# The first feed-forward of a two-block kernel: root refinement moved into the long product, left unit's low half ahead of the weight sums, halves of the token sums one chunk later, seven pairs with sums in place of eight

## The reference, cut to what matters

```python
x = x + h                                      # x: (256, 1024)
h = rms_norm(x, norm2_g)                       # row root of mean square, gain norm2_g
x = x + jnp.square(jax.nn.relu(h @ w_ff1)) @ w_ff2      # w_ff1: (1024, 4096), w_ff2: (4096, 1024)
```

## Time and profile before

| | |
|---|---|
| median of three runs | 1223.64 us |
| the profiled execution | 1223.52 us |
| its span | 1221.7 us |
| mean granted clock of TensorE | 0.998 |
| PE busy | 1207.2 us, 99% |
| POOL busy | 862.1 us, 71% |
| ACT busy | 679.6 us, 56% |
| DVE busy | 673.9 us, 55% |
| first product, second product of the first block | 334.8 to 431.1 us, 431.1 to 517.7 us |

### The profile page before, as it was taken

How to read it: one execution, slowest core, us unless ns; L and a number is a source line. 1 busy time by engine, 2 the same in 40 slices (tenths; PEclk the granted TensorE clock), 3 DMA queues, 4 the chain that set the end, 5 groups by cost and what they waited for, 6 DMA issues and landing times.

```text
span 1221.7 us, 18529 instructions
## 1 busy us (share of the span) xinstructions
PE 1207.2 (99%) x7367; PEld 1044.6 (85%) x7367; DVE 673.9 (55%) x1161; ACT 679.6 (56%) x915; POOL 862.1 (71%) x373
## 2 busy tenths in 40 slices
PE   9999999999998999999999999999999999999998
PEld 8987888888887887799999888888879878888877
DVE  6847456341356689756662154536653674544855
ACT  6873757655476566446554464444556666444533
POOL 7977468659876720867579788883776648998194
PEclk9999999999999999999999999999999999999999
DMA  9755355437655655655466776665658435676461
GB/s 304 204 165 171 105 153 170 141 106 223 205 155 147 184 184 195 206 164 159 127 175 214 255 202 184 195 188 160 213 160 283 139 109 170 189 206 189 165 214 69
DMA packets 147773, 218.33 MB, mean 179 GB/s; under 512 B 9392, under 2 KB 79591, under 8 KB 147687
## 3 DMA queue, kind: packets, MB, share of 16 engines
q1 hardware_dynamic: 144295, 209.92, 56.6%
q10 hardware_dynamic: 3392, 7.23, 1.8%
HBM read 216.08 MB, written 1.05 MB: 178 GB/s over the span
## 4 chain that ended last, share of the span: by engine, by line
PE 81%; DVE 10%; POOL 4%; ACT 3%; issue 1%; DMA 0%; SPq 0%; DVEq 0%; ACTq 0%
PE acc L2273 14%; PE acc L2310 8%; PE acc L2312 8%; PE acc L2311 8%; PE acc L2280 7%; PE pm L2326 5%; POOL wlo L640 4%; PE acc L2317 4%; PE acc L2319 4%; PE acc L2320 4%; DVE wlo L1698 2%; PE acc L2239 2%; DVE XT L1726 2%; PE acc L2240 2%; PE acc L2241 2%
## 5 line engine op out<-in xcount | busy, mean ns | idle before, releaser
L640 POOL TENSOR_TENSOR wlo<-raw,whi 128x1024 fp32r<-128x1024 f32 (+4 forms) x366 | 856.8, 2374 | 347.1 <-ACT whi L654 237.2
L654 ACT ACTIVATE whi<-raw 128x1024 fp32r<-128x1024 f32 (+4 forms) x404 | 402.2, 1020 | 211.2 <-PE acc L2280 50.1
L2273 PE MATMUL acc<-XT,whi 128*128 128x512 f32 x960 | 231.7, 393 | 4.5 <-DVE f1r L1741 4.3
L2273 PEld LDWEIGHTS acc<-XT,whi 128*128 128x128 f32 x960 | 177.4, 189 | 40.2 <-DVE f1r L1741 4.7
L2280 PEld LDWEIGHTS acc<-XT,wlo 128*128 128x128 f32 x960 | 123.4, 191 | 4.8
L2280 PE MATMUL acc<-XT,wlo 128*128 128x256 f32 x960 | 124.8, 283 | 0.0
L2310 PE MATMUL acc<-whi,XT 128*128 128x512 f32 (+4 forms) x296 | 112.6, 380 | 0.1
L2317 PE MATMUL acc<-XT,whi 128*128 128x256 f32 x392 | 111.9, 285 | 0.0
L2319 PE MATMUL acc<-XT,whi 128*128 128x256 f32 x392 | 110.9, 283 | 0.0
L2320 PE MATMUL acc<-XT,wlo 128*128 128x256 f32 x392 | 110.9, 283 | 0.0
L2312 PE MATMUL acc<-whi,XT 128*128 128x512 f32 (+4 forms) x296 | 110.0, 372 | 0.0
(11 more groups left out here) (537 smaller groups left out, 2290.8 us busy)
## 6 DMA issues: line engine op xcount, KB each, us to landing
raw<-in_w_in SPq DMA_DIRECT2D x68, 512.0 KB, 4.3
raw<-in_w_ff SPq DMA_DIRECT2D x64, 512.0 KB, 3.8
raw<-in_w_gate SPq DMA_DIRECT2D x44, 512.0 KB, 3.8
raw<-in_w_up SPq DMA_DIRECT2D x44, 512.0 KB, 3.9
raw<-in_w_down SPq DMA_DIRECT2D x44, 512.0 KB, 3.8
raw<-in_w_in_mix SPq DMA_DIRECT2D x36, 512.0 KB, 3.7
raw<-in_w_branch SPq DMA_DIRECT2D x16, 512.0 KB, 4.0
raw<-in_w_out_mix SPq DMA_DIRECT2D x16, 512.0 KB, 3.4
```

Of the source, the lines that this page charges most:

```text
L640: nc.gpsimd.tensor_tensor(piece(wlo, u), piece(raw, u), piece(whi, u).bitcast(F32), ALU.subtract).then_inc(S["w_lo"], 1)
L654: return nc.scalar.activation(out_, in_, func, **k)
L2273: T.matmul(acc[:, n % 2, f, :], piece(whi, u)[:, i, f * P:(f + 1) * P], XT[:, :, k, :], start=k == 0, stop=False)
```

## The change

Four edits, all but one in the first block's feed-forward:

- `SUMS["f2"]` has seven pairs, (2, 4, 5, 7, 9, 10, 12), where it had eight, (2, 3, 5, 6, 8, 9, 11, 12).
- In the loop over the chunks of the first product, `split_sums` of a chunk stands behind the two instructions that read out the next chunk.
- The refinement of the root leaves this loop and stands in the second product, behind the low halves of pair 3.
- In `mixed_lows`, for all three stages, the low half of the left unit is made ahead of the weight sums. Since a left unit's `raw` slot is still read by the sums then, SP waits for one low half more before it reloads such a slot.

```diff
-SUMS = {"f2": (2, 3, 5, 6, 8, 9, 11, 12), "fd0": (2, 3, 5), "fd1": (2, 3, 5)}
+SUMS = {"f2": (2, 4, 5, 7, 9, 10, 12), "fd0": (2, 3, 5), "fd1": (2, 3, 5)}
...
-                    sp_.wait_ge(S["w_lo"], u - RAW + 1)
+                    sp_.wait_ge(S["w_lo"], u - RAW + (2 if u - RAW + 1 in sum_rights else 1))
...
-            def mixed_lows(stage):
+            def mixed_lows(stage, between=None):
...
                     if p not in SUMS[stage]:
                         low_half(left)
                         low_half(right)
+                        if between is not None and p == SUMS[stage][0] + 1:
+                            between()
                         continue
                     g = SUM_FIRST[stage] + SUMS[stage].index(p)
+                    low_half(left)
                     v.wait_ge(S["w_hi"], right + 1)
...
-                    low_half(left)
                     low_half(right, slice(1, UK))
...
+            made = None
             for c in range(DFF // HW):
...
-                if c == 7:
-                    v.wait_ge(S["rstd"], 2)
-                    link(half_variance(0, NT, ss[:, 0:NT], D, 1e-6))
-                    refine_columns(0, NT)
...
                 link(V.tensor_copy(f1r[:], accB(f"f1_{c}", 1)))
                 V.tensor_tensor(f1r[:], accB(f"f1_{c}", 0), f1r[:], ALU.add).then_inc(evac_at(f"f1_{c}")[0], 1)
+                if made:
+                    split_sums(*made)
                 v.wait_ge(S["f1_hi"], c + 1)
                 made = token_sums("f2", c, f1s) if c in SUMS["f2"] else None
                 V.tensor_tensor(FFlo[:, 2 * c:2 * c + 2, :], f1s, FFhi[:, 2 * c:2 * c + 2, :].bitcast(F32),
                                 ALU.subtract).then_inc(S["f1_lo"], 1)
-                if made:
-                    split_sums(*made)
-            mixed_lows("f2")
+            if made:
+                split_sums(*made)
+
+            def squared_roots():
...
+            mixed_lows("f2", squared_roots)
```

More of the change, by code:

```diff
@@ L1733, in _ @@
                     v.wait_ge(S["f1_hi"], c)
-                if c == 7:
-                    v.wait_ge(S["rstd"], 2)
-                    link(half_variance(0, NT, ss[:, 0:NT], D, 1e-6))
-                    refine_columns(0, NT)
-                    link(V.tensor_tensor(rs[:, 8:8 + NT], rs[:, 0:NT], rs[:, 0:NT], ALU.mult))
-                    link(V.tensor_scalar(rs[:, 8 + NT:8 + 2 * NT], rs[:, 8:8 + NT], -1.0, None, ALU.mult))
                 link(V.tensor_copy(f1r[:], accB(f"f1_{c}", 1)))
                 V.tensor_tensor(f1r[:], accB(f"f1_{c}", 0), f1r[:], ALU.add).then_inc(evac_at(f"f1_{c}")[0], 1)
+                if made:
+                    split_sums(*made)
                 v.wait_ge(S["f1_hi"], c + 1)
@@ L1745, in _ @@
                                 ALU.subtract).then_inc(S["f1_lo"], 1)
-                if made:
-                    split_sums(*made)
-            mixed_lows("f2")
+            if made:
+                split_sums(*made)
+            def squared_roots():
+                v.wait_ge(S["rstd"], 2)
+                link(half_variance(0, NT, ss[:, 0:NT], D, 1e-6))
+                refine_columns(0, NT)
+                link(V.tensor_tensor(rs[:, 8:8 + NT], rs[:, 0:NT], rs[:, 0:NT], ALU.mult))
+                link(V.tensor_scalar(rs[:, 8 + NT:8 + 2 * NT], rs[:, 8:8 + NT], -1.0, None, ALU.mult))
+            mixed_lows("f2", squared_roots)
             def folded(t, c, bank):
```

## The result

The changed kernel has a median of 1214.57 us over six runs (1214.50 to 1214.66), the kernel before 1223.68 beside it (1223.36 to 1224.08): 9.1 us less, a ratio of 0.9926, 95% interval 0.9913 to 0.9938. The profiled execution took 1214.64 us with a span of 1212.5.

What follows compares the result with a forecast made beforehand. PE was taken to bound the kernel, busy 99%, losing 10.55 us in two products to waits for late DVE. First product -6.41 and second -3.16 gave -9.6: 1213.9 profiled, 1214.0 median, range 1213.0 to 1216.5.

Steps and rivals of the forecast that it cites:

- two large terms: The first product was to lose 6.41 us and the second 3.16 us, the latter with 0.68 of extra matmuls included.
- The split costs nothing: First product: DVE's split needs 1.3 us and fits in the 1.91 us in which it waits for ACT.
- First product, -6.41: First product: 6.41 us lost to PE's long wait, slow matmuls behind it and a later wait would all go.
- both causes: First product: DVE's 1.5 to 3 us of lag from the sums and the refinement's 3.33 us together broke the allowed lateness.
- The distance of 4.1 us: First product: DVE may be 4.1 us late (5.57 - 1.4) before PE notices.
- Slow clock, 1.71 of it: First product: 16 matmuls behind the long wait took 5.36 us for 3.65, 1.71 lost at granted clock 0.50.
- The refinement costs 1.44 in its new place: Second product: 3.33 us less a 2.04 first instruction read as a wait for POOL, plus 0.15; upper bound 3.33.
- Seven pairs, +0.68, and 66.3 for all thirteen: Second product: 0.68 us more matmuls, thirteen pairs in 66.3 us against 69.42, with 0.3 waited in pair 12.
- Left low half first, and SP's wait: nothing: Pairs with sums: the 1.14 us delay of the sums stays hidden with 0.4 to spare; the later slot costs nothing.
- The rival of the transfers: Second product: second transfers land late, so pairs 10 and 12 wait; 2.4 us more, 1216.4; chance 0.12.
- the slower one: Three stages: the left low half's 1.14 us shows in all 13 sums pairs, 14.8 us, so 1228.8; chance 0.04.
- fd0 and fd1, within 0.3: Stages fd0 and fd1: no waits listed, same count, reordered lows only; change 0, within 0.3 us either way.

Runs made afterwards that it cites:

- s_split: The kernel before with only the split of the token sums moved behind the next chunk's read-out: 1217.61 us, ratio 0.9948.
- t_refback: The changed kernel with the refinement put back ahead of chunk 7 of the first product: 1214.75 us, 0.9925 of the kernel before.
- u_twoparts: The kernel before with two edits, the split a chunk later and seven pairs with sums: 1214.45 us, ratio 0.9923.
- u_delay: The changed kernel with eight extra read-out copies on DVE ahead of chunk 7's read-out in the first product: 1217.97 us, 0.9952 of the kernel before.
- s_refine: The kernel before with only the refinement moved into the second product, behind pair 4's low halves: 1222.02 us, ratio 0.9986.
- t_eight: The changed kernel with the old eight pairs with sums, the refinement behind pair 4: 1218.17 us, 0.9954 of the kernel before.
- t_column: The kernel before with the refinement's first step as two one-column (128x1) instructions instead of one of two columns: 1222.75 us, ratio 0.9993.
- s_seven: The kernel before with only seven pairs with sums for eight in the second product: 1219.65 us, ratio 0.9965.
- u_pool: The changed kernel with POOL resuming only behind the last sums' low halves of each stage: 1215.14 us, 0.9929 of the kernel before.
- t_oldlow: The changed kernel with the left unit's low half behind the weight sums again and SP's old wait: 1214.28 us, 0.9922 of the kernel before.
- u_six: The changed kernel with sums in six pairs of the second product, never two in a row: 1214.43 us, 0.9923 of the kernel before.
- s_lows: The kernel before with only the left unit's low half made first and SP's longer wait: 1223.28 us, ratio 0.9996.

## Why the prediction was right

The forecast was 1214.0 with 1213.3 to 1214.7 around it, the time 1214.57. Its two large terms came true within 0.1 us, one of them for a reason that was half wrong. Step by step:

- **The split costs nothing.** Shown: its 1.3 us lie in ACT's gap, 0.59 of it is left, and s_split gains 6.2 alone.
- **First product, -6.41.** It is -6.44 (47.32 to 40.88). The prediction gave it to both causes together, and there it was wrong: the split's move alone removes 6.29 (s_split), and t_refback and u_twoparts, which keep the refinement in the loop, lose only 0.44. The distance of 4.1 us is 3.9 by u_delay, and t_refback says the same, where 4.07 us on DVE make PE 0.17 late.
- **Slow clock, 1.71 of it.** The clock fell to 0.50 behind waits of 3.55, 3.57, 2.44 and 2.48, and stayed at 1.00 behind those of 1.06 (s_refine), 1.67 (t_eight), 1.75 (u_delay) and 1.84 (s_refine). Since no such wait is left, none of it is left.
- **The refinement costs 1.44 in its new place.** Shown: 1.46 (437.96 to 439.42). That the 2.04 of its first instruction is a stand for POOL is shown by t_column, and s_seven shows what the step left out: later 128x2 instructions can stand too, so in the loop it cost 5.2 there.
- **Seven pairs, +0.68, and 66.3 for all thirteen.** 66.27. DVE started pair 2 at 4.14 (4.1 forecast), pair 4 at 14.5 (14.5), pair 10 at 46.2 (46.4) and pair 12 at 55.7 (55.9) after PE. The wait in pair 12 is 0.28 (0.3), and u_pool shows POOL as its cause. That the old eight pairs were too much for DVE is shown by t_eight; whether their number or their order was, is not.
- **Left low half first, and SP's wait: nothing.** Shown by t_oldlow. The rival of the transfers did not come, nor did the slower one: DVE's short waits inside pairs with sums are those in pairs 5 and 10.
- **fd0 and fd1, within 0.3.** The fold of fd0 comes 9.3 earlier than before and the span is 9.2 shorter, so 0.1.

The two products gave 9.6, as summed. The profiled execution missed its 1213.9 by 0.7: PE entered the first product's steady part 0.27 later than before (in the first ten us of the kernel, which the change doesn't touch), 0.1 came behind, and around the span lie 2.14 us in place of 1.82. None of the three was in the sum. The first two are smaller than what executions of the kernel before differ by (1223.36 to 1224.08). The third is no scatter: all six executions of the changed kernel have 2.10 to 2.17 around the span, u_pool's four have the same, and the kernel before, t_oldlow, u_six and u_twoparts have 1.8. No run shows why, so small differences are better read from spans.

No version beats the changed kernel by more than this: t_oldlow's 1214.28 is 0.3 lower with the same span. The plainest one with the whole gain, within 0.1 us of the span, is u_twoparts.

## What to carry to other kernels

Keep two figures for each stage: how late the helping engine is, chunk by chunk, and how late it may be before the main one notices. Only work that goes past that distance costs. Several causes share one wait, and so the gains of edits made alone do not add (12.6 against 9.1). Then take the smallest edit that brings the lateness under the distance. Before you use an engine's free time, ask which small instructions would have to stand there until another engine's whole operation ends.

## What the hardware showed that was not expected

- DVE instructions of 128x2 elements in SBUF, both TENSOR_SCALAR and TENSOR_TENSOR with two inputs in SBUF, stood until POOL's current operation ended: 2.04, 1.74, 2.31, 1.50, 1.45 and 0.93 us where they take 0.16. Those of 128x1 beside the same work took 0.10 to 0.23 each and never stood. The Trainium skill, page "SBUF — State Buffer", section "SBUF: two separate sides", which the prediction names, has this lock for VectorE instructions with two SBUF inputs and for those in a two-port mode. The trace agrees for the first form, and for TENSOR_SCALAR of 128x2 it shows the same stand. That the single column escapes is from t_column.
- With a granted clock of 0.50, 1.2 GHz of 2.4, 16 matmuls took 5.36 to 5.38 us for 3.65 behind waits of 2.44 to 3.55, so 1.7 more. In s_lows, behind a wait of 3.57, they took 6.25. Behind waits of up to 1.84 the clock stayed at 1.00.
- In u_delay 14 matmuls of 128 columns took 0.23 us each at the start, twice the usual, while the granted clock of that stretch reads 1.00: a pace is read from the matmuls' starts, and the clock's column is a help.
